# Where the rows of the normed activations begin in on-chip memory: 1088-byte rows against 1152-byte rows, all tiles behind them shifted

## The chip, the cores and the metric

The kernel runs on one core of a Trainium2 chip. The metric is the device time of one execution in microseconds (us). The kernel before was run three times: 1245.53, 1247.48 and 1249.95 us, median 1247.48 us. On-chip memory (SBUF) has 128 partitions; a tile occupies the same byte range in each of them, and this document is about where those ranges begin.

## The reference

The program computes four blocks in a row on an input of 256 tokens by 1024 channels, all in fp32. Cut to what matters here:

```
x = x + conformer_conv(rmsnorm(x))      # 1024 -> 2048, conv of width 31, 1024 -> 1024
x = x + swiglu(rmsnorm(x))              # 1024 -> 2 x 2816 -> 1024
x = x + dilated_attention(rmsnorm(x))
x = x + swiglu(rmsnorm(x))
cond = silu(c); mod = cond @ ada_w + ada_b        # shifts, scales, gates
x = x + g1 * (even_mixer(rmsnorm(x) * (1 + sc1) + sh1) @ w_out)
x = x + g2 * swiglu(rmsnorm(x) * (1 + sc2) + sh2)
x = x + g1' * (odd_mixer(rmsnorm(x) * (1 + sc1') + sh1') @ w_out')
x = x + g2' * swiglu(rmsnorm(x) * (1 + sc2') + sh2')
```

with `swiglu(h, wg, wu, wd) = (silu(h @ wg) * (h @ wu)) @ wd`. Nearly all arithmetic is in sixteen matrix products of activations with weights.

## The kernel before

**Layout of the data.** Activations lie transposed: channels on the 128 partitions, tokens along the row. A tensor of 1024 channels is 8 rows (`kt` = 0 to 7) of 256 tokens. Every fp32 operand of a big product is split into a high and a low part in the matrix unit's fp32r format: `HH` and `HL` for normed activations (two sets each, `[128, 8, TW]`), `GH` and `GL` for the gated activations of the feed-forward (`[128, 22, 256]`), `whi` and `wlo` for weights (six buffers each, one unit of eight 128x128 blocks per buffer). For a block of weights and a row of activations the TensorE queue runs three matmuls (line 528): weights high with activations high, weights high with activations low, weights low with activations high. The names in the profile put the activation first: `ps<-HH,whi`, `ps<-HL,whi`, `ps<-HH,wlo`, then the next block. I call these three a triple; the weights are the stationary operand and the row of activations the moving one.

**Products.** In order: pw1 (16 output tiles), pw2 (8), gu0 (44), dn0 (8), mixd (18), outd (8), gu1 (44), dn1 (8), mixe (23), oute (8), gu2 (44), dn2 (8), mixo (12), outo (8), gu3 (44), dn3 (8). The `gu` products are the gate and up projections, the `dn` products are the down projections and read `GH`/`GL` in 22 triples per output tile; all the others read `HH`/`HL` in 8 triples per tile (6 for outd). In mixe, gu2, mixo and gu3 the moving row has 258 columns instead of 256, since two columns behind the tokens carry the shift of the modulation (hence rows that are wider than 256). In six of mixd's tiles the roles are swapped (weights moving, activations stationary). The first two to four output tiles of a product ("lead") are interleaved: for each `kt` all lead tiles use the same row, so that 6 to 12 matmuls in a row read it; from then on tile follows tile, and each row is used for three matmuls. Orders differ in two products: outd goes through its rows as 0, 2, 4, 1, 3, 5 and oute as 0, 1, 4, 5, 2, 6, 3, 7.

**The other engines.** SyncE's queue streams the weights (`raw`, five buffers of 512 KB); ScalarE rounds each unit to `whi` (line 865), VectorE subtracts to `wlo` (line 1274), one unit after the other, five units ahead of TensorE. Between these, ScalarE and VectorE take the results out of PSUM, compute norms, gates and attention, and VectorE accumulates the modulation's sums (`aacc`). Each `whi` waits until TensorE has finished with the buffer.

**Placement.** Tiles are placed one behind the other in the order in which they are declared (`sb(...)`, lines 390 to 468), each rounded up to a multiple of 32 bytes; a group in a `with ExitStack() as st:` gives its place back at the end of the block, so that the next group begins where it began. The first buffer, `raw0`, begins at byte 16512, 128 beyond a multiple of 512, and so, because they are all multiples of 512 bytes long, does every `raw`, `whi`, `wlo` buffer, `X`, and `HH`, `HL`. With `TW` = 272 the rows of `HH` and `HL` are 1088 bytes apart. Beyond a multiple of 256 the rows then begin as follows (the pattern repeats after four):

```
row kt             0    1    2    3    4    5    6    7
HH, HL before    128  192    0   64  128  192    0   64   (bytes beyond a multiple of 256)
GH, GL before     64 for every row (base 181824, rows of 1024 bytes)
```

The ones among the small tiles that the change touches: `epsb`, `epse` and eight `bcol` tiles of one column each, 32 bytes apiece. VectorE writes a `bcol` from PSUM (lines 1499, 1618) and ScalarE or VectorE add it as a bias.

Of the kernel before, what the change touches and what calls it, by code (L numbers as in the profile page):

```python
# [7 lines left out]
F32 = mybir.dt.float32  # L8
# [5 lines left out]
P = 128  # L14
T = 256
# [2 lines left out]
KF = 22  # L18
EPS = 1e-6
UW = T + 28  # L20
TW = T + 16
NB = P + T
NR = 24
NEG = -1e30
# [360 lines left out]
def program(nc, wall, ada, x_in, vec_in, wq_in, row_in, rel_in, k128, kdist, koh, kmask, kbias, scratch, uscr, out):  # L385
    with ExitStack() as ctx:
        S = Signals(lambda name: ctx.enter_context(nc.semaphore("s_" + name)))

        def sb(name, shape, dt=F32, stack=ctx):
            return stack.enter_context(nc.sbuf_tensor(name, shape, dt))  # L390
# [3 lines left out]
        whi = [sb(f"whi{i}", [P, BLK * P], F32R) for i in range(RING)]  # L394
        wlo = [sb(f"wlo{i}", [P, BLK * P], F32R) for i in range(RING)]
        X = sb("X", [P, KD, T])
        HH = [sb(f"HH{i}", [P, KD, TW], F32R) for i in range(2)]
        HL = [sb(f"HL{i}", [P, KD, TW], F32R) for i in range(2)]
        RST = [sb(f"RST{i}", [P, T]) for i in range(2)]
# [2 lines left out]
        dist = sb("dist", [P, 384])  # L402
        vec, row = sb("vec", [P, NVEC]), sb("row", [P, NROW])
        MOD, GM, FG, cond = sb("MOD", [P, 96]), sb("GM", [P, 4, 8]), sb("FG", [P, 8]), sb("cond", [P, 8])
        epsb, epse = sb("epsb", [P, 1]), sb("epse", [P, 1])
        gqk, sc, rcol, lamt = sb("gqk", [P, 3]), sb("sc", [P, 8]), sb("rcol", [P, 2]), sb("lamt", [P, 2, 64])
        bcol = [sb(f"bcol{i}", [P, 1]) for i in range(8)]
        TMP = [sb(f"tmp{i}", [P, T]) for i in range(9)]
        TN = [sb(f"tn{i}", [P, T]) for i in range(2)]
        TS = [sb(f"ts{i}", [P, T]) for i in range(2)]  # L410
# [35 lines left out]
        SQC, SQD = sb("SQC", [P, T]), sb("SQD", [P, T])  # L446
        TS2 = [sb(f"tt{i}", [P, T]) for i in range(2)]
        with ExitStack() as st:
            GH, GL = sb("GH", [P, KF, T], F32R, st), sb("GL", [P, KF, T], F32R, st)
        with ExitStack() as st:  # L450
            oQ, oK, oV = sb("oQ", [P, 8, T], F32, st), sb("oK", [P, 4, T], F32, st), sb("oV", [P, 2, 256], F32, st)
# [7 lines left out]
        def V(name, i=0):  # L459
            c = VCOL[name] + i  # L460
            return vec[:, c:c + 1]

        def gain(i, nt):
            return (V("nm0", nt), V("nf0", nt), V("nm1", nt), V("nf1", nt), FG[:, nt:nt + 1], GM[:, 1, nt:nt + 1],
                    GM[:, 2, nt:nt + 1], GM[:, 3, nt:nt + 1])[i]
# [29 lines left out]
        def tensor_program():  # L495
# [41 lines left out]
            def total(i):  # L537

                pe.wait_ge(S.k128, 48)
                pe.wait_ge(S.sqa, 6 * (i + 1))  # L540
                pe.e.matmul(bank[7][:, 0:T], ones[:, :], SQA[:, :], start=True, stop=False)
                pe.wait_ge(S.sq, 8 * (i + 1))
                pe.then_inc(pe.e.matmul(bank[7][:, 0:T], ones[:, :], SQB[:, :], start=False, stop=True), S.tot)

            def norm_ready(i):
                def ready(kt):
                    pe.wait_ge(S.hl, 8 * i + kt + 1)
                    if i >= 4:
                        pe.wait_ge(S.sh, 2 * (i - 3))
                return ready  # L550
# [18 lines left out]
            def convolution():  # L569
# [17 lines left out]
                def after(nt):  # L587
# [8 lines left out]
                    if nt == 4:  # L596
# [4 lines left out]

                product("pw1", HH[NORM_SET[0]], HL[NORM_SET[0]], T, norm_ready(0), after,
                        lambda kt: total(0) if kt == KD - 1 else None)
# [17 lines left out]
                pe.then_inc(square, S.lnt)  # L621
                product("pw2", HH[LN_SET], HL[LN_SET], T, lambda kt: pe.wait_ge(S.lnl, kt + 1))

            def feed_forward(f):
# [6 lines left out]

                product(f"gu{f}", HH[NORM_SET[i]], HL[NORM_SET[i]], T + 2 if f >= 2 else T, norm_ready(i), after)
                product(f"dn{f}", GH, GL, T, lambda kt: pe.wait_ge(S.gl, KF * f + kt + 1),
# [15 lines left out]
            def dilated():  # L649
# [41 lines left out]
                def before(kt):  # L691
                    for w, hs in BEFORE_D.get(kt, ()):
                        step(w, hs)

                product("mixd", HH[NORM_SET[2]], HL[NORM_SET[2]], T, norm_ready(2), after)

                product("outd", HH[YD_SET], HL[YD_SET], T,
                        lambda kt: pe.wait_ge(S.dhl, 3 * (2 * (kt % 2) + 1) + kt // 2 + 1), None, before)
# [18 lines left out]
            def slotted(slot):  # L717

                def after(nt):
                    if nt == 1:  # L720
                        slot(2)
                    slot(2 * nt + 1)
                return dict(middle=lambda nt: slot(2 * nt), after=after)
# [7 lines left out]
            def even():  # L731
# [54 lines left out]
                def slot(s):  # L786
                    if s == 1:
                        total(4)
                        pe.wait_ge(S.sqa2, 6)
                        pe.wait_ge(S.amod, 3)  # L790
                        pe.e.matmul(bank[6][:, 0:T], ones[:, :], SQC[:, :], start=True, stop=False)
                        pe.wait_ge(S.sq2, 8)
                        pe.then_inc(pe.e.matmul(bank[6][:, 0:T], ones[:, :], SQD[:, :], start=False, stop=True), S.tot2)
                    project(TE, s)
                    if s == 16:
                        pe.wait_ge(S.twb, 1)
                        pe.wait_ge(S.sd, NORM_RST[4] + 2)
                    for w, k in AFTER_E.get(s, ()):
                        step(w, k)
# [6 lines left out]

                product("mixe", HH[NORM_SET[4]], HL[NORM_SET[4]], T + 2, norm_ready(4), **slotted(slot))
                product("oute", HH[YE_SET], HL[YE_SET], T, ready, None, lambda kt: slot(46 + PROD["oute"].order.index(kt)))
# [51 lines left out]
        def scalar_program():  # L860
# [3 lines left out]
            def act(o, i, func, sem, **kw):  # L864
                ac.then_inc(ac.e.activation(o, i, func, **kw), sem)  # L865
# [24 lines left out]
            def norm_high(i, nt):  # L890
# [3 lines left out]
                if i >= 4:  # L894
                    ac.wait_ge(S.gn, 3 if i < 6 else i - 2)
                act(HH[NORM_SET[i]][:, nt, 0:T], X[:, nt, :], ACT.Copy, S.hh, scale=gain(i, nt))

            def square(i, nt):
                streamed(i, nt)
                if nt in (0, KD - 1):  # L900
                    ac.wait_ge(S.tot, i)
                    act((SQB if nt else SQA)[:, :], X[:, nt, :], ACT.Square, S.sq)
                else:
                    m = 6 * i + nt - 1
                    ac.wait_ge(S.sqa, max(m - 1, 0))
                    act(TS[m % 2][:, :], X[:, nt, :], ACT.Square, S.sq)

            def square2(nt):
# [3 lines left out]
                else:  # L912
                    ac.wait_ge(S.sqa2, max(nt - 2, 0))
                    o = TS2[(nt - 1) % 2]
                act(o[:, :], X[:, nt, :], ACT.Square, S.sq2, scale=V("fin", nt))

# [352 lines left out]
        def vector_program():  # L1269
# [9 lines left out]
            def stt(o, a, s, b, op, op2, sem):  # L1279
                dv.then_inc(dv.e.scalar_tensor_tensor(out=o, in0=a, scalar=s, in1=b, op0=op, op1=op2), sem)  # L1280
# [34 lines left out]
            def norm_low(i, nt):  # L1315
                dv.wait_ge(S.hh, 8 * i + nt + 1)
                stt(HL[NORM_SET[i]][:, nt, 0:T], X[:, nt, :], gain(i, nt), HH[NORM_SET[i]][:, nt, 0:T].bitcast(F32),
                    ALU.mult, ALU.subtract, S.hl)
# [44 lines left out]
            def residual(name, i, scale, op, before=None):  # L1363
# [7 lines left out]
                for nt in range(p.tiles):  # L1371
# [12 lines left out]
                    else:  # L1384
                        dv.wait_ge(S.hl, 8 * j + nt + 1)
                    stt(X[:, nt, :], ps[:, 0:T], scale(nt), X[:, nt, :], op, ALU.add, S.ev)
                    if i is not None and nt == p.tiles - 1:
# [732 lines left out]
```

## Time and profile before

| | us |
|---|---|
| median of 3 runs (lowest to highest) | 1247.48 (1245.53 to 1249.95) |
| the profiled execution's own time | 1249.51 |
| its span, first to last instruction | 1248.2 |
| TensorE matmul busy / VectorE / ScalarE / GpSimd | 1186.6 / 926.3 / 657.7 / 80.1 |
| granted TensorE clock, mean share of full speed | 0.988 |

A busy matmul unit is not one at its peak: one matmul's record here lasts about 280 ns, but a new one starts every 113 to 120 ns, since they are pipelined. What counts is therefore the distance from one start to the next. It is read either from a timeline (starts to 10 ns) or from a view of one line's instructions over a stretch, which gives a count and the first and last start: the distance of the last from the first, divided by the count less one, is the time of one triple.

### The profile page before, as it was taken

The numbers are of one execution on the slowest core, as the hardware profiler recorded it, in microseconds if no ns is written. First come the engines' busy times: TensorE is split into PE (matmuls) and PEld (weight loads), VectorE is DVE, ScalarE is ACT, GpSimd is POOL, SyncE is SP. The second block draws the span as 40 slices with busy tenths as digits, with TensorE's granted clock in tenths as the row PEclk, the third lists the DMA queues.
The fourth block names the chain that finished last, engine by engine and source line by source line (L and its number), as shares of the span: only waits on it lengthen the run. The fifth ranks groups of instructions, "written<-read, shape, count | busy, mean of one in ns | idle before, by whom it ended". The sixth has DMA issues, their size and how long they took to land.

```text
span 1248.2 us, 24814 instructions
## 1 busy us (share of the span) xinstructions
PE 1186.6 (95%) x9914; PEld 1130.0 (91%) x9914; DVE 926.3 (74%) x1761; ACT 657.7 (53%) x1143; POOL 80.1 (6%) x91
## 2 busy tenths in 40 slices
PE   7898999999998999999997889999999899999999
PEld 7777999999987999999986779999998778999999
DVE  6646798878777888788788768888885565766653
ACT  6336654445445644446455776544445776544441
POOL 2010000001000100002100011000000222000000
PEclk9999999999999999999999999999999999999999
DMA  7862697878753588778744335887776432666561
GB/s 269 239 178 70 229 311 257 265 264 289 262 190 118 179 268 252 251 239 287 261 135 125 111 113 196 276 255 249 254 289 210 140 111 85 218 182 182 181 201 68
DMA packets 81270, 257.78 MB, mean 207 GB/s; under 512 B 9016, under 2 KB 22020, under 8 KB 81156
## 3 DMA queue, kind: packets, MB, share of 16 engines
q1 hardware_dynamic: 75396, 250.36, 60.9%
q10 hardware_dynamic: 5760, 5.83, 1.9%
q8 instruction: 79, 1.29, 0.4%
q14 instruction: 35, 0.29, 0.1%
HBM read 253.49 MB, written 2.67 MB: 205 GB/s over the span
## 4 chain that ended last, share of the span: by engine, by line
PE 79%; DVE 8%; ACT 4%; issue 3%; DMA 1%; POOL 1%; ACTq 0%; DVEq 0%; POOLq 0%
PE ps L528 71%; PE ps L579 2%; DVE wlo L1274 2%; PE ps L638 1%; PE ps L646 1%; PE ps L637 1%; PE ps L642 1%; DMA UR<-uscr 1%; DVE X L1280 1%; ACT whi L865 1%; DVE aacc L1280 1%; ACT oS L865 1%; ACT HH L865 1%; DVE HL L1280 1%; PE ps L560 1%
## 5 line engine op out<-in xcount | busy, mean ns | idle before, releaser
L528 PE MATMUL ps<-HH,whi 128*128 128x256 f32 (+1 forms) x2152 | 619.7, 288 | 17.8 <-DVE wlo L1274 8.2
L528 PE MATMUL ps<-HL,whi 128*128 128x256 f32 (+1 forms) x2152 | 611.4, 284 | 0.0
L528 PE MATMUL ps<-HH,wlo 128*128 128x256 f32 (+1 forms) x2152 | 610.7, 284 | 0.0
L865 ACT ACTIVATE whi<-raw 128x1024 fp32r<-128x1024 f32 (+1 forms) x364 | 382.3, 1054 | 340.5 <-PE ps L528 325.7
L1274 DVE TENSOR_TENSOR wlo<-raw,whi 128x1024 fp32r<-128x1024 f32 (+1 forms) x364 | 441.8, 1221 | 45.7 <-ACT whi L865 45.3
L528 PEld LDWEIGHTS ps<-HH,whi 128*128 128x128 f32 x2152 | 411.8, 191 | 34.9 <-issue 24.7
L528 PEld LDWEIGHTS ps<-HH,wlo 128*128 128x128 f32 x2152 | 412.6, 192 | 0.0
L528 PEld LDWEIGHTS ps<-HL,whi 128*128 128x128 f32 x2152 | 411.4, 191 | 0.4
L528 PE MATMUL ps<-GH,whi 128*128 128x256 f32 x704 | 195.6, 278 | 0.6 <-DVE bcol L1499 0.5
L528 PE MATMUL ps<-GL,whi 128*128 128x256 f32 x704 | 195.0, 277 | 0.0
L528 PE MATMUL ps<-GH,wlo 128*128 128x256 f32 x704 | 195.0, 277 | 0.0
L1280 DVE SCALAR_TENSOR_TENSOR aacc<-araw,cond,aacc 128x512 f32<-128x512 f32 x168 | 132.1, 786 | 3.4
L528 PEld LDWEIGHTS ps<-GH,whi 128*128 128x128 f32 x704 | 132.7, 189 | 2.1 <-DVE bcol L1499 0.9
L528 PEld LDWEIGHTS ps<-GL,whi 128*128 128x128 f32 x704 | 132.2, 188 | 0.0
L528 PEld LDWEIGHTS ps<-GH,wlo 128*128 128x128 f32 x704 | 132.2, 188 | 0.0
L1805 POOL TENSOR_TENSOR SQA<-SQA,ts 128x256 f32<-128x256 f32 x48 | 41.0, 855 | 717.7 <-ACT ts L865 717.1
L1498 DVE TENSOR_TENSOR tmp<-ps,RST 128x256 f32<-128x256 f32 x88 | 37.1, 422 | 48.3 <-PE ps L528 47.5
L1274 DVE TENSOR_TENSOR tmp<-ps,RST 128x256 f32<-128x256 f32 x104 | 43.6, 420 | 36.3 <-PE ps L528 35.8
L865 ACT ACTIVATE tmp<-tmp,bcol 128x256 f32<-128x256 f32 x74 | 36.9, 500 | 32.3 <-DVE bcol L1618 30.6
L865 ACT ACTIVATE GH<-tmp 128x256 fp32r<-128x256 f32 x88 | 35.6, 404 | 23.2 <-DVE tmp L1274 18.1
L1274 DVE TENSOR_TENSOR GL<-tmp,GH 128x256 fp32r<-128x256 f32 x88 | 36.8, 418 | 1.9 <-ACT GH L865 1.9
L1280 DVE SCALAR_TENSOR_TENSOR X<-ps,MOD,X 128x256 f32<-128x256 f32 x32 | 15.2, 478 | 30.7 <-PE ps L528 30.7
(220 smaller groups left out, 937.9 us busy)
## 6 DMA issues: line engine op xcount, KB each, us to landing
raw<-wall SPq DMA_DIRECT2D x363, 512.0 KB, 4.3
araw<-ada SPq DMA_DIRECT2D x96, 512.0 KB, 4.7
UR<-uscr ACTq DMA_DIRECT2D x32, 142.0 KB, 3.8
oBB<-kbias SPq DMA_DIRECT2D x16, 192.0 KB, 2.5
aTB<-scratch SPq DMA_DIRECT2D x12, 128.0 KB
uscr<-U ACTq DMA_DIRECT2D x8, 143.5 KB, 4.9
out<-X SPq DMA_DIRECT2D x8, 128.0 KB, 2.9
aTB<-scratch SPq DMA_DIRECT2D x12, 64.0 KB
```

What stands on the lines that cost most here:

```text
L528: ins = pe.e.matmul(o, l, r, start=(kt == p.order[0] and i == 0), stop=(kt == p.order[-1] and i == 2))
L560: ins = pe.e.matmul(bank[6][32 * i:32 * i + 32, :], ones[:, 0:32], aacc[(4 * b + i) % AACC][:, :], start=True, stop=True)
L579: ins = pe.e.matmul(bk[32 * r:32 * r + 32, 0:T], DG[j % 3][:, 8 * r + m, :], UR[j % 3][:, r, 4 * m:4 * m + T], start=(m == 0), stop=(m == 7))
L637: pe.e.matmul(bk[:, 0:128], q[:, 0:128], k[:, 0:128], start=True, stop=True)
L638: return pe.e.matmul(bk[:, 128:384], q[:, 128:256], k[:, 0:256], start=True, stop=True)
L642: ins = pe.e.transpose(bk[:, i * P:(i + 1) * P], s[:, i * P:(i + 1) * P], ident[:, :])
L646: pe.e.matmul(o, v(0), pt[:, 0:256], start=True, stop=False)
L865: ac.then_inc(ac.e.activation(o, i, func, **kw), sem)
L1274: dv.then_inc(dv.e.tensor_tensor(o, a, b, op), sem)
L1280: dv.then_inc(dv.e.scalar_tensor_tensor(out=o, in0=a, scalar=s, in1=b, op0=op, op1=op2), sem)
L1498: dv.e.tensor_tensor(t[:, :], ps[:, 0:T], rooted(name)[:, :], ALU.mult)
L1805: po.then_inc(po.e.tensor_tensor(o, a, b, op), sem)
```

## The change

The rows of `HH` and `HL` become 64 bytes longer: `TW` goes from 272 to 288 elements, 1152 bytes. A tile `half` of 64 bytes, which nothing reads or writes, is declared ahead of `HH`; another, `halfg`, ahead of `GH` and `GL`, in their own group. The ten one-column tiles are merged into two, `eps2` and `bcols`, and used by the same names through slices. No instruction is added, removed or moved on any engine, and no wait or semaphore changes.

```diff
-TW = T + 16
+TW = T + 32
...
         X = sb("X", [P, KD, T])
+        sb("half", [P, 16])
         HH = [sb(f"HH{i}", [P, KD, TW], F32R) for i in range(2)]
         HL = [sb(f"HL{i}", [P, KD, TW], F32R) for i in range(2)]
...
-        epsb, epse = sb("epsb", [P, 1]), sb("epse", [P, 1])
+        eps2, bcols = sb("eps2", [P, 2]), sb("bcols", [P, 8])
+        epsb, epse = eps2[:, 0:1], eps2[:, 1:2]
+        bcol = [bcols[:, i:i + 1] for i in range(8)]
         gqk, sc, rcol, lamt = sb("gqk", [P, 3]), sb("sc", [P, 8]), sb("rcol", [P, 2]), sb("lamt", [P, 2, 64])
-        bcol = [sb(f"bcol{i}", [P, 1]) for i in range(8)]
...
         with ExitStack() as st:
+            sb("halfg", [P, 16], F32, st)
             GH, GL = sb("GH", [P, KF, T], F32R, st), sb("GL", [P, KF, T], F32R, st)
```

## Rows read from the trace of the kernel before

**Rows 1.** The page: busy time by engine, and shares of the chain by line

```profile
PE 1186.6 (95%) x9914; PEld 1130.0 (91%) x9914; DVE 926.3 (74%) x1761; ACT 657.7 (53%) x1143; POOL 80.1 (6%) x91
...
PE ps L528 71%; PE ps L579 2%; DVE wlo L1274 2%; PE ps L638 1%; PE ps L646 1%; PE ps L637 1%; PE ps L642 1%; DMA UR<-uscr 1%; DVE X L1280 1%; ACT whi L865 1%; DVE aacc L1280 1%; ACT oS L865 1%; ACT HH L865 1%; DVE HL L1280 1%; PE ps L560 1%
```

**Rows 2.** Waits, whole run: engine, line, releaser: total us, times, longest

```profile
ACT whi L865 <- PE ps L528: 325.7, 222, 10.0
```

**Rows 3.** Groups by line and shape: count | busy us, mean ns | idle before

```profile
L528 PE MATMUL ps<-HH,whi 128*128 128x256 f32 x1168 | 333.6, 286 | 14.8 <-DVE wlo L1274 8.2 <-DVE HL L1274 5.2 <-DVE X L1280 1.2
...
L528 PE MATMUL ps<-HH,whi 128*128 128x258 f32 x984 | 286.2, 291 | 3.0 <-DVE bcol L1618 2.0 <-DVE X L1280 1.0
...
L528 PE MATMUL ps<-GH,whi 128*128 128x256 f32 x704 | 195.6, 278 | 0.6 <-DVE bcol L1499 0.5 <-DVE tmp L1274 0.2
```

**Rows 4.** Line 528 in gu0, 142 to 249 us: count, ns min/median/max, first to last start

```profile
L528 PE MATMUL ps<-HL,whi x303: 279/282/283, 141.7 to 248.9; 128*128 128x256 f32 x152
```

**Rows 5.** The same in gu3, 1078 to 1178 us

```profile
L528 PE MATMUL ps<-HH,whi x280: 280/282/285, 1077.8 to 1178.0; 128*128 128x258 f32 x140
```

**Rows 6.** The same in dn1, 551.5 to 609 us

```profile
L528 PE MATMUL ps<-GH,whi x170: 276/276/276, 551.3 to 608.7; 128*128 128x256 f32 x170
```

**Rows 7.** The same in dn2's first six tiles, 894.3 to 940.5 us

```profile
L528 PE MATMUL ps<-GL,whi x131: 281/281/281, 894.1 to 940.0; 128*128 128x256 f32 x131
```

**Rows 8.** The same in dn2's last two tiles, 942 to 956 us

```profile
L528 PE MATMUL ps<-GH,wlo x40: 276/276/283, 942.0 to 955.7; 128*128 128x256 f32 x40
```

**Rows 9.** Timeline of TensorE in pw1's lead: start us, duration us, instruction

```profile
15.40 0.28 PE L528 MATMUL ps<-HH,whi 128*128 128x256 f32 x1
...
16.08 0.28 PE L528 MATMUL ps<-HH,whi 128*128 128x256 f32 x1
...
17.50 0.28 PE L528 MATMUL ps<-HH,whi 128*128 128x256 f32 x1
...
18.92 0.28 PE L528 MATMUL ps<-HH,whi 128*128 128x256 f32 x1
```

**Rows 10.** The same in outd's lead, rows 1, 3, 5 in turn

```profile
404.61 0.28 PE L528 MATMUL ps<-HH,whi 128*128 128x256 f32 x1
...
405.32 0.28 PE L528 MATMUL ps<-HH,whi 128*128 128x256 f32 x1
...
406.02 0.28 PE L528 MATMUL ps<-HH,whi 128*128 128x256 f32 x1
...
406.73 0.29 PE L528 MATMUL ps<-HH,whi 128*128 128x256 f32 x1
```

**Rows 11.** The same in outo's lead, row 5 behind a wait

```profile
1035.48 0.28 PE L528 MATMUL ps<-HL,whi 128*128 128x256 f32 x1
...
1036.30 0.28 PE L528 MATMUL ps<-HH,wlo 128*128 128x256 f32 x1
```

**Rows 12.** The same in gu3's lead (258 columns), rows 1 and 3

```profile
1058.91 0.28 PE L528 MATMUL ps<-HH,whi 128*128 128x258 f32 x1
...
1059.98 0.28 PE L528 MATMUL ps<-HH,whi 128*128 128x258 f32 x1
...
1061.07 0.28 PE L528 MATMUL ps<-HH,whi 128*128 128x258 f32 x1
...
1062.15 0.28 PE L528 MATMUL ps<-HH,whi 128*128 128x258 f32 x1
```

**Rows 13.** The same in one later tile of gu3

```profile
1073.45 0.28 PE L528 MATMUL ps<-HH,whi 128*128 128x258 f32 x1
...
1074.17 0.28 PE L528 MATMUL ps<-HH,whi 128*128 128x258 f32 x1
...
1074.55 0.28 PE L528 MATMUL ps<-HH,whi 128*128 128x258 f32 x1
...
1075.97 0.28 PE L528 MATMUL ps<-HH,whi 128*128 128x258 f32 x1
```

**Rows 14.** Instructions that write or read HH, bcol, and line 579

```profile
L865 ACT ACTIVATE HH<-X,vec x32: 490/509/513, 4.4 to 422.6; 128x256 fp32r<-128x256 f32 x32
...
L1499 DVE COPY bcol<-ps x88: 141/148/151, 773.5 to 1185.7; 128x1 f32<-128x1 f32 x88
...
L579 PE MATMUL ps<-UR,DG x512: 376/379/472, 36.6 to 98.1; 128*32 128x256 f32 x171
```

## The prediction

> **What bounds the kernel now.** First the page: TensorE is busy 95% of the span, and 71% of the chain that ended last is line 528, the matmuls of the big products [rows 1]. ScalarE waits 325.7 us in all for TensorE to free a weight buffer, and hardly for anything else in that line [rows 2], so the weight stream runs ahead, and a faster or slower matmul goes straight into the time. The reader is to see that no other engine needs to be looked at for a change that moves no instruction.
>
> Then the groups by shape. A matmul on HH has a mean of 286 ns at 256 columns and 291 at 258, one on GH 278 [rows 3], though HH and GH matmuls at 256 columns do the same work. The means are of pipelined records, so I read distances between starts. In gu0 302 triples take 107.2 us, 355.0 ns each: 118.3 ns a matmul [rows 4]. In dn1 169 triples take 57.4 us, 339.6 ns each: 113.3 a matmul [rows 6]; dn0 and dn3 show the same. In gu3 279 triples take 100.2 us: 119.7 a matmul [rows 5]. So HH matmuls are 4 to 5 ns slower than GH ones, and there are many of them: 3 x 1168 at 256 columns and 3 x 984 at 258 [rows 3].
>
> **What the placement has to do with it.** GH is not fast everywhere. In dn2's first six tiles, same tiles, same places, 130 triples take 45.9 us, 117.7 ns a matmul, every record 281 ns [rows 7]; behind the wait that follows them the records are 276 ns again [rows 8]. A stream over equally placed rows thus has a fast rate (113.3) and a slow one (117.7), and keeps the one it falls into. Next, which placements know the fast rate. In a product's lead several matmuls in a row read one row of HH. In pw1's lead the last six on row 3 (64 bytes beyond a multiple of 256) take 0.68 us, the first two starts shown, 113.3 each [rows 9]; the twelve on row 4 (128 beyond) take 1.42 us, 118.3 each, and the twelve on row 5 (192 beyond) again 1.42 us, and these never come down [rows 9]. Behind a wait, where the stream starts afresh, row 5 in outo runs 7 matmuls in 0.82 us, 117.1 [rows 11], also slow. I find thirteen such runs of six or more on rows that lie 192 beyond, from pw1's to outo's (the two shown), and none reaches 113.3; on rows 64 beyond, and on GH and GL, which also lie 64 beyond, both rates occur. So what counts here is the place within 256 bytes, not within 128: 64 can be fast, 192 is slow.
>
> **The change part by part.** Nothing is added to any queue; everything is in the addresses.
>
> HH and HL move by 64 bytes and get rows of 1152 bytes: 128 + 64 = 192, and 1152 is 4 x 256 + 128, so the rows lie 192, 64, 192, 64, ... beyond a multiple of 256. All are 64 beyond a multiple of 128, as announced.
>
> GH and GL: HH and HL add 4 x 8 x 64 = 2048 bytes, `half` 64, the merged columns give back 7 x 32 + 32 = 256, `halfg` adds 64: 1920 bytes in all. 181824 + 1920 = 183744, which is 192 beyond a multiple of 256. They too stay 64 beyond a multiple of 128, but leave the place where the fast rate was seen. The weights stay where they are.
>
> *Term 1, the gated products.* Fast today are dn0, dn1, dn3 (8 x 22 x 3 = 528 matmuls each) and dn2's last two tiles (132): 1716. If rows 192 beyond have only the slow rate, each costs 117.7 - 113.3 = 4.4 ns more [rows 6, 7]: +7.6 us, all on the path. Bounds: if they keep the fast rate 0, and -1.7 if dn2's 396 slow ones become fast too. I take +7.6, by the thirteen runs.
>
> *Term 2, HH at 256 columns.* 3504 matmuls, at 118.3 today [rows 4]. outd's order happens to give exactly the new sequence: rows 1, 3, 5 lie 192, 64, 192 beyond. Its lead runs the 18 matmuls in 2.12 us, 117.8 each [rows 10]; the run on the row at 64 stays slow when it comes from a slow one. So -0.5 ns each: -1.8 us. Bounds: 113.3 for all, -17.5 us, and 118.3 again, 0.
>
> *Term 3, HH at 258 columns.* 2952 matmuls, at 119.7 today [rows 5]. Leads: row 1 (192) nine in 1.07 us, 118.9; row 3 (64) nine in 1.08, 120.0 [rows 12]. In a later tile, each row used three times: row 1 and the one behind it 120.0, row 3 126.7 (0.38 us for three), the twelve behind it 118.3 [rows 13]. Taking the odd rows at lead rates gives 119.4; with row 3 at 126.7 and the other three at 119 it gives 120.9. Neither has the new steps between rows, so I take the middle, about 120.1: +1.0 us. Bounds: 114.2 (113.3 x 258 / 256), -16.2 us, and 120.9, +3.5.
>
> *The rest.* The 144 matmuls of mixd with swapped roles read HH as weights, too few for a microsecond. ScalarE writes to HH took 490 to 513 ns over all eight rows [rows 14], so its rows' places show no cost there worth a bound over 32 x 0.02 = 0.7 us, and TensorE hides it. VectorE's copies to bcol took 141 to 151 ns at eight different places [rows 14]; packing them costs nothing visible, hidden as well except in the mixers. The taps' moving rows start at 16-byte steps and have a median of 379 with a minimum of 376 [rows 14]: moving them, and the attention's tiles, is worth at most 3 ns x 512 = 1.5 us either way; I take 0.
>
> *A rule against the rows.* The fast rate is 113.3 ns for 256 columns, the slow one 117.7, at unchanged shape and clock [rows 6, 7]. The Trainium skill (TensorE: Matmul & The Clock Gate, "Part 2: What happens when you issue a matmul") gives the gap between warm matmuls as columns / 2.4 GHz plus about 2.5 ns, 109.2 ns here, and says that loading the next weights takes nothing from the running matmul, since each has its own read port. By that no address matters and the change would do nothing; the two rates in this trace speak against it.
>
> *Sum.* 7.6 - 1.8 + 1.0 = +6.8 us. Against the profiled execution's 1249.5 that is 1256.3. The median of the runs is 2.0 lower, so I forecast **1254.3 us**.
>
> **Rivals.**
>
> *A, the forecast: 192 beyond is slow, the gated products lose the fast rate.* Own range: term 1 of 6.5 to 8, term 2 of -4 to 0, term 3 of -1.2 to +3.5, rest within 1.5: +1 to +12 at most, 1249 to 1259.5. Chance 0.53.
>
> *B, 128 is what counts.* Then the trouble of HH is only the step from a row at 0 to one at 64 beyond 128, and with equal rows all run like GH: -17.5 - 16.2 - 1.7 = -35 us, 1212. For it: GH's rows all equal, HH's not. Against it: the thirteen runs at 192, long enough to settle, that did not. Chance 0.17.
>
> *C, addresses hardly matter.* The two rates come from how the stream restarts after a wait, as in dn2 where the place did not change [rows 7, 8]. Then nothing moves but which stretch is slow: between -1.7 and, if one more dn turns slow, +2.3 us; 1247.5. Against: the ordered differences within one lead [rows 9]. Chance 0.17.
>
> *D, half a win.* Alternating rows fall into the fast rate on every second row: (113.3 + 117.7) / 2 = 115.5 at 256 columns, -2.8 x 3504 = -9.8 us, as much again in half at 258, -5, with the gated products' +7.6: -7, 1240. For: runs on row 3 come down within six matmuls [rows 9]. Against: outd [rows 10], and only three matmuls a row. Chance 0.13.
>
> **How the numbers follow.** A measurement of this kernel tells a change from none beyond about 0.3%, 3.7 us. Faster by more: B 0.17, D 0.10, together 0.27. Within: C 0.15, D 0.03, the low end of A 0.05: 0.23. Slower by more: A 0.48, C 0.02: 0.50. The range leaves out B: from D's 1240 less its spread to the top of A, 1236 to 1261.
>
> **What would show it.** In dn0, dn1, dn3 the records of line 528: 281 ns and triples of 353 ns if A or D is right, 276 and 340 if B or C. In gu0 and gu1 triples of 353 to 354 by A, 340 by B, 355 by C, about 346 by D. In gu3 about 360 by A. The prediction is wrong if GH at 192 beyond keeps 276 ns, or if the alternating rows of HH come below 350 ns a triple.

## The result and the profile after

| | before | after |
|---|---|---|
| median of the runs, us | 1247.56 (20 runs, 1238.97 to 1254.93) | 1252.22 (20 runs, 1246.47 to 1256.83) |
| profiled execution, us | 1249.51 | 1252.52 |
| its span, us | 1248.2 | 1251.2 |
| mean granted clock in it | 0.988 | 0.989 |

After over before is 1.0044, with a 95% interval of 1.0025 to 1.0062: 3.1 to 7.7 us slower. The forecast difference of +6.8 us lies inside; the middle, +5.5 us (0.44% of 1247.6), is 1.3 less.

The page of after first: busy time of each engine, and shares of the chain. TensorE grew by 2.3 us and still makes 71% of the chain with the line of the big products (531 now, 528 before) [rows 1].

```profile
PE 1188.9 (95%) x9914; PEld 1131.2 (90%) x9914; DVE 927.6 (74%) x1761; ACT 657.1 (53%) x1143; POOL 80.7 (6%) x91
...
PE ps L531 71%; DVE wlo L1277 2%; PE ps L582 1%; ACT whi L868 1%; PE ps L641 1%; PE ps L649 1%; PE ps L640 1%; DVE X L1283 1%; DMA uscr<-U 1%; PE ps L645 1%; DMA UR<-uscr 1%; DVE aacc L1283 1%; ACT oS L868 1%; ACT HH L868 1%; DVE HL L1283 1%
```

The waits of after (engine, line, releaser: total us, times, longest). ScalarE waits 5.4 us more for TensorE to free a weight buffer than in [rows 2], so the weight stream has as much slack as before, and slower matmuls are not hidden.

```profile
ACT whi L868 <- PE ps L531: 331.1, 223, 10.2
```

The groups of after by line and shape (busy us, mean ns of one, idle before). Against [rows 3], HH at 256 columns went from 286 to 285 ns, at 258 from 291 to 292, GH from 278 to 280: three small moves in two directions.

```profile
L531 PE MATMUL ps<-HH,whi 128*128 128x256 f32 x1168 | 332.3, 285 | 14.8 <-DVE wlo L1277 8.0 <-DVE HL L1277 5.2 <-DVE X L1283 1.3
L531 PE MATMUL ps<-HH,whi 128*128 128x258 f32 x984 | 287.1, 292 | 3.1 <-DVE bcols L1621 2.0 <-DVE X L1283 1.1
...
L531 PE MATMUL ps<-GH,whi 128*128 128x256 f32 x704 | 197.4, 280 | 0.6 <-DVE bcols L1502 0.5 <-DVE tmp L1277 0.2
```

The means mix stretches, so again line 531 by stretch, one of its three matmuls each (count, ns min/median/max, first to last start): gu0, dn1, dn2's first six tiles, gu3.

```profile
L531 PE MATMUL ps<-HH,wlo x307: 277/277/279, 141.7 to 248.8; 128*128 128x256 f32 x154
...
L531 PE MATMUL ps<-GH,whi x164: 279/279/279, 551.3 to 608.9; 128*128 128x256 f32 x164
...
L531 PE MATMUL ps<-GL,whi x129: 278/279/279, 896.6 to 941.8; 128*128 128x256 f32 x129
...
L531 PE MATMUL ps<-HH,wlo x278: 278/282/289, 1077.8 to 1177.8; 128*128 128x258 f32 x139
```

gu0: 306 triples in 107.1 us, 350.0 ns each, where [rows 4] had 355.0. dn1: 163 triples in 57.6 us, 353.4, where [rows 6] had 339.6. dn2: 128 triples in 45.2 us, 353.1, as in [rows 7]. gu3: 277 triples in 100.0 us, 361.0, where [rows 5] had 359.1.

The granted clock does not explain the two rates: in before it was full (1.00, the number behind the count in brackets) in dn2's slow stretch and in the fast one behind it, and so it was in after's gu0 and dn1.

```profile
894.30:940.00 45.70, 45.70 (x390) 1.00 0.76 266
941.30:956.00 14.70, 14.70 (x133) 1.00 0.62 201
```

The same read for every product, as the mean distance between starts of neighbouring matmuls, gives what I call the account below. Only distances under 140 ns are taken, so stalls are left out, and the difference of the means is multiplied by the number of these distances (2097 for the 2112 gated matmuls, some 3380 for the 3504):

| term | predicted | ns a matmul, before to after | us |
|---|---|---|---|
| 1, gated products, 2112 matmuls | +7.6 | 114.2 to 117.8 | +7.5 |
| 2, HH at 256 columns, 3504 | -1.8 | 118.2 to 116.9 | -4.5 |
| 3, HH at 258 columns, 2952 | +1.0 | 119.9 to 120.3 | +1.3 |
| sum | +6.8 | | +4.3 |

The spans differ by 3.0 us, so -1.3 us are left. Some -0.5 of them is mixd's 144 matmuls with swapped roles, which the prediction had put at nothing: they went from 118.0 to 113.7 ns each. The other -0.8 lies in stalls and small products, and no row names a cause for it.

### The profile page after: what moved, and what is told of

The parts are those of the page before. It is cut to its first block, busy times and chain, and to the rows that moved or that the text cites. A ratio compares the mean times of both kernels' runs of the same rounds, so it can differ in the third digit from the quotient of the medians.

```text
span 1251.2 us, 24814 instructions
## 1 busy us (share of the span) xinstructions
PE 1188.9 (95%) x9914; PEld 1131.2 (90%) x9914; DVE 927.6 (74%) x1761; ACT 657.1 (53%) x1143; POOL 80.7 (6%) x91
## 4 chain that ended last, share of the span: by engine, by line
PE 78%; DVE 9%; ACT 5%; issue 3%; DMA 2%; POOL 1%; ACTq 0%; DVEq 0%; POOLq 0%
PE ps L531 71%; DVE wlo L1277 2%; PE ps L582 1%; ACT whi L868 1%; PE ps L641 1%; PE ps L649 1%; PE ps L640 1%; DVE X L1283 1%; DMA uscr<-U 1%; PE ps L645 1%; DMA UR<-uscr 1%; DVE aacc L1283 1%; ACT oS L868 1%; ACT HH L868 1%; DVE HL L1283 1%
## 5 line engine op out<-in xcount | busy, mean ns | idle before, releaser
L868 ACT ACTIVATE whi<-raw 128x1024 fp32r<-128x1024 f32 (+1 forms) x364 | 382.3, 1054 | 345.2 <-PE ps L531 331.1
L868 ACT ACTIVATE tmp<-tmp,bcols 128x256 f32<-128x256 f32 x74 | 36.9, 500 | 32.3 <-DVE bcols L1621 30.7
```

## Experiments

The theory, in the form that the experiments led to: what decides is the distance, modulo 256 bytes, between a row that TensorE reads and the weights, which lie 128 beyond a multiple of 256. The prediction had spoken of the row's place alone, and the expectations call the common part "theory 1". A place allows certain rates, and at a restart, behind a wait, a stream falls into one of them. Rival one: only the restart decides, and all four gated products turned slow by accident. Rival two: the row's own place counts, whatever the weights'. Places are given as bytes beyond a multiple of 256.

### The gated rows alone, taken back and added

e1_gated_back is after with GH and GL returned to 64.

```diff
-            sb("halfg", [P, 16], F32, st)
+            sb("halfg", [P, 48], F32, st)
```

> The changed kernel with 128 bytes more ahead of GH and GL, so that they lie 64 beyond a multiple of 256 again; HH and HL as in the change (192, 64, 192, 64, ...). Theory 1 (the place within 256 bytes sets the rate): records of the dn products back at 276 ns, triples of 340 ns, at least in dn0, dn1, dn3; gu0 and gu1 stay at about 350 ns a triple as in the changed kernel. The time is 7.7 us under the changed kernel's: 1244.5, some 3 us under the kernel before. Theory 2 (the slow rate is an accident of how a stream restarts): no connection with the 128 bytes, dn stays at 353 ns a triple, 1252. Rival 3 (it is the place within 128 bytes, or the change's other tiles): the same as theory 2, 1252.

e2_gated_alone is before with GH and GL moved to 192 and nothing else.

```diff
+            sb("halfg", [P, 32], F32, st)
             GH, GL = sb("GH", [P, KF, T], F32R, st), sb("GL", [P, KF, T], F32R, st)
```

> The kernel before with 128 bytes ahead of GH and GL and nothing else: they lie 192 beyond a multiple of 256. Theory 1: dn0 to dn3 at 353 ns a triple throughout, all other products unchanged (355 in gu0, 359 in gu3), time +7.6 us: 1255. Theory 2: no change, 1247.5.

Measured: e1 1247.61 us, ratio to before 1.0008 [0.9983, 1.0034]; e2 1255.82 us, ratio 1.0072 [1.0047, 1.0097]. Line 531 of e1 in dn0, then line 529 of e2 in gu0 and in dn1 (columns as above):

```profile
L531 PE MATMUL ps<-GH,whi x148: 275/276/277, 259.8 to 309.7; 128*128 128x256 f32 x148
```

```profile
L529 PE MATMUL ps<-HH,wlo x302: 279/282/283, 141.8 to 248.7; 128*128 128x256 f32 x151
...
L529 PE MATMUL ps<-GL,whi x114: 278/279/280, 559.8 to 599.7; 128*128 128x256 f32 x114
```

e1: 147 triples in 49.9 us, 339.5: the fast rate came back with the place, in all four gated products. e2: HH untouched (301 triples in 106.9 us, 355.1), dn1 at 113 triples in 39.9 us, 353.1, and all four gated products at 117.8 ns. By the account, e2 has +7.5 in term 1 and 0.1 or less elsewhere; e1 has -3.8 in term 2, -1.7 in term 1 (dn2 was fast throughout) and +0.9 in term 3. Term 1 is thus shown both ways. e2's median agrees with the expected 1255. e1's is 3 us above the expected 1244.5: its account of -4.6 us against before is there in its profiled execution (1243.95 us at a granted clock of 0.989, 5.6 less than before's), and not in its median; the last section comes back to that.

### What the distance is measured from

e3_all_128 moves everything from the raw weights on by 128 bytes, the weights included; e4_weights_128 moves the weights whi and wlo alone (a second shift restores the rest modulo 256).

```diff
 e3, ahead of raw:      + sb("shift", [P, 32])
 e4, ahead of whi:      + sb("shift", [P, 32])
 e4, ahead of X:        + sb("shift2", [P, 32])
```

> The kernel before with 128 bytes ahead of the first buffer, so that every tile lies 128 further, the weights too (0 beyond a multiple of 256 instead of 128, GH 192 instead of 64). Theory 1a (the distance between the row and the block of weights counts, within 256 bytes): every product as before, dn 340 ns a triple, 1247. Theory 1b (the row's own place counts): dn at 353 ns, 1255.

> The kernel before with 128 bytes ahead of the weights' split buffers and 128 behind them: only whi and wlo move within 256 bytes (0 beyond instead of 128), every row of activations stays. Theory 1a (distance to the weights): dn slow, 353 ns a triple, 1255. Theory 1b (the row's own place): dn 340 ns, 1247.

Measured, one execution each: e3 1244.33 us, e4 1257.97. Line 529 of e3 in dn1, then line 530 of e4 in dn0 and in dn1:

```profile
L529 PE MATMUL ps<-GH,wlo x119: 275/276/277, 559.8 to 599.9; 128*128 128x256 f32 x119
```

```profile
L530 PE MATMUL ps<-GH,whi x143: 279/279/279, 259.7 to 309.9; 128*128 128x256 f32 x143
...
L530 PE MATMUL ps<-GL,whi x148: 276/276/276, 559.7 to 609.7; 128*128 128x256 f32 x148
```

In e3 GH lies at 192, as in after, and is fast (118 triples in 40.1 us, 339.8), as in the other three gated products (dn2's last tile excepted, 117.8 ns a matmul). In e4 GH lies at 64, as in before, and dn0 is slow (142 triples in 50.2 us, 353.5), as are dn2 and dn3. With before and after, that makes all four combinations of two places of the row and two of the weights, and the rate goes with the distance between them: rival two falls. The last line belongs to neither side: e4's dn1 took the fast rate (147 triples in 50.0 us, 340.1) at the slow distance.

### Every row of the 256-column products at 64

e5_rows_1024 is before, with the 256-column products going through views with rows of 1024 bytes at 64 in the same buffers.

```diff
+        HN, LN = ([b[:, 48:48 + KD * T].rearrange("p (k t) -> p k t", t=T) for b in B] for B in (HHB, HLB))
...
-                product("pw1", HH[NORM_SET[0]], HL[NORM_SET[0]], T, norm_ready(0), after,
+                product("pw1", NH[0], NL[0], T, norm_ready(0), after,
```

(HHB and HLB are the buffers of HH and HL without rows; NH and NL are these views for products 0 to 3 and the old rows for the wider ones. The lines that write HH and HL use the same views.)

> The kernel before, where the products with 256 columns (pw1, pw2, gu0, mixd, outd, gu1, oute, outo) address HH and HL with rows of 1024 bytes that all begin 64 beyond a multiple of 256, in the same memory; the products with 258 columns keep rows of 1088 bytes, and no tile moves. Theory 1 (the distance of the row from the block of weights, within 256 bytes, sets which rates there are, and 64 knows the fast one): 340 ns a triple wherever the fast rate is caught, so up to 4.9 ns x 3504 matmuls = 17 us less: 1230 to 1236; if a stream is caught in the slow rate, 353 there, and the gain of that product is 0.5 ns a matmul. Rival (HH is slower than GH for another reason, such as its writers or its being renewed during the product): 353 to 355, 1246.

> The kernel with 1024-byte rows at 64 once more, for the rates of its streams in a second profiled execution. The two later kernels with the same rows had gu0 at 117.5 ns a matmul and gu1 at 113.4, so the fast rate is caught by chance: each of gu0, gu1, pw2 and outd at 113.4 or 117.7, not all of them fast as the first time; time between 1233 (all fast) and 1243.

Measured: e5 1240.75 us, ratio 0.9948 [0.9924, 0.9971], faster than both kernels, but 5 us above the expected 1230 to 1236; e12, the same kernel again, one execution, 1238.2. The page and the waits of e5, line 532 of e5 in gu0, then that of e12 in gu0 and in dn2:

```profile
PE 1170.0 (95%) x9914; PEld 1112.8 (90%) x9914; DVE 925.7 (75%) x1761; ACT 657.6 (53%) x1143; POOL 80.8 (7%) x91
```

```profile
ACT whi L869 <- PE ps L532: 306.6, 214, 10.2
```

```profile
L532 PE MATMUL ps<-HH,wlo x289: 276/276/276, 141.8 to 239.7; 128*128 128x256 f32 x145
```

```profile
L532 PE MATMUL ps<-HH,wlo x289: 276/276/276, 141.8 to 239.8; 128*128 128x256 f32 x145
...
L532 PE MATMUL ps<-GL,whi x126: 281/281/281, 885.8 to 930.0; 128*128 128x256 f32 x126
```

288 triples in 97.9 us: 339.9 in gu0, the rate that only the gated products had before. Not every product got it: pw1 had 115.6 ns a matmul, oute 117.1 and outo 116.9, which is why term 2 falls short of the 17 us that were possible. TensorE's busy time falls by 16.6 us against [rows 1] and ScalarE's wait by 19.1 against [rows 2]; the account gives -14.0 us in term 2 and -1.7 in term 1, and the two spans differ by 15.2 (1248.2 to 1233.0). The medians differ by only 4.3 (1245.06 to 1240.75) and the ratio says 6.5: the profiled execution, 1234.31 us, lies near the lowest of the 12 runs, 1233.21. e12 keeps gu0 fast but has dn2 slow at 125 triples in 44.2 us, 353.6, and outd at 117.6.

### A map of places

e6_gated_map gives GH and GL another place in each gated product (0, 32, 96, 128); e7_all_64 puts all rows at 64, with rows of 1280 bytes for 258 columns; e8_places_258 is e7 with the 258-column products at 128, 192, 32, 0 and the gated ones at 160, 224, 64, 192; e11_192_for_258 is e7 with the 258-column rows at 192. To make room, e7, e8 and e11 also merge the one-column tiles and place some scratch tiles over others, and e8 has two load buffers for the modulation instead of three; their times are therefore less clean than their rates.

```diff
 e6: +            GHV, GLV = ([b[:, o:o + KF * T].rearrange("p (k t) -> p k t", t=T) for o in (48, 56, 8, 16)] for b in (GHB, GLB))
 e7: +TW = T + 64
 e8: +        AT = {4: 0, 5: 16, 6: 40, 7: 32}
 e11: -        sb("half", [P, 48])
 e11: +        sb("half", [P, 16])
 e11: -        HN, LN = ([b[:, 0:0 + KD * T]...
 e11: +        HN, LN = ([b[:, 32:32 + KD * T]...
```

> The kernel before with GH and GL read and written at another place in each feed-forward: dn0 at 0, dn1 at 32, dn2 at 96, dn3 at 128 bytes beyond a multiple of 256 (the weights lie 128 beyond). Theory 1: each place has rates of its own; by the lead's runs of HH rows 0 gives about 356 ns a triple, 128 about 358 to 360; 32 and 96 were never seen, between 340 and 360. Rival (only the step between rows matters, not the constant place): all four at 340.

> All moving rows 64 beyond a multiple of 256: the products with 258 columns get rows of 1280 bytes, those with 256 columns rows of 1024 bytes, GH and GL as before. The room for it comes from merging the one-column tiles and from placing four scratch rows of the sums and one of the dilated attention's buffers over scratch that is free at that time. Theory 1: the products with 256 columns as in the run with 1024-byte rows, 340 to 353 ns a triple. For 258 columns it does not say which rate a constant row gives: between 342.5 (340 x 258 / 256) and the lead rows' 357 to 360; so 1213 to 1236. Rival: nothing gained, 1246.

> Rows of 258 columns with a constant place, 1280 bytes apart: mixe at 128, gu2 at 192, mixo at 32, gu3 at 0 beyond a multiple of 256 (the run with all at 64 had 120.8 ns a matmul in gu2 and gu3). GH and GL in dn0 at 160, dn1 at 224, dn2 at 64, dn3 at 192. One of the modulation's three load buffers is left out to make room, which may cost VectorE waits but not TensorE's rate. Theory 1: with 258 columns each matmul leaves the next one two columns further off, so that no place keeps a fast rate: 118.5 to 121 everywhere. Rival: some place knows 114.2. For the dn products: dn3 353 ns a triple, dn2 340 or 353, the other two between 350 and 360.

> The two best places together: 256-column rows 1024 bytes apart at 64 beyond a multiple of 256, GH and GL at 64, and 258-column rows 1280 bytes apart at 192, where gu2 took 118.8 ns a matmul against 119.8 in the kernel before. Theory 1: gu2 and gu3 118.8, mixe and mixo 119 to 120, the others 113.3 where the fast rate is caught and 117.7 where not; 3 us less than the run with 1024-byte rows, 1238. Rival (the 118.8 was one more accident of a restart): gu2 or gu3 above 119.5, 1241 or more.

Measured: e6 1255.06 us and e8 1251.5, one execution each; e7 1243.25, ratio 0.9979 [0.9952, 1.0005], so not clear of before and above the expected 1213 to 1236; e11 1239.35, ratio 0.9951 [0.993, 0.9973]. The line of the products in each: e6 in dn0 and dn3; e7 in gu0, gu1 and gu3; e8 in gu2 and gu3; e11 in gu0 and gu3.

```profile
L529 PE MATMUL ps<-GL,whi x142: 279/281/285, 259.7 to 309.9; 128*128 128x256 f32 x142
...
L529 PE MATMUL ps<-GL,whi x148: 280/283/287, 1191.8 to 1244.7; 128*128 128x256 f32 x148
```

```profile
L535 PE MATMUL ps<-HL,whi x270: 281/281/281, 149.8 to 244.8; 128*128 128x256 f32 x135
...
L535 PE MATMUL ps<-HH,wlo x230: 276/276/276, 441.8 to 519.6; 128*128 128x256 f32 x115
...
L535 PE MATMUL ps<-HH,wlo x222: 280/283/289, 1089.8 to 1169.9; 128*128 128x258 f32 x111
```

```profile
L535 PE MATMUL ps<-HH,whi x170: 277/282/283, 779.8 to 840.0; 128*128 128x258 f32 x170
...
L535 PE MATMUL ps<-HH,wlo x219: 282/283/283, 1079.8 to 1159.7; 128*128 128x258 f32 x110
```

```profile
L535 PE MATMUL ps<-HH,wlo x270: 280/281/282, 149.7 to 244.8; 128*128 128x256 f32 x135
...
L535 PE MATMUL ps<-HH,whi x225: 277/283/286, 1079.8 to 1159.8; 128*128 128x258 f32 x113
```

As triples: e6 356.0 at 0 and 359.9 at 128; e7 353.2 in gu0, 339.7 in gu1, both at 64, and 362.4 in gu3; e8 356.2 at 192 and 366.5 at 0; e11 353.5 in gu0 and 357.1 in gu3. Mean distances, ns a matmul, with all rows of a product at one place and the weights at 128:

| place | 256 columns | 258 columns |
|---|---|---|
| 0 | 118.7 | 122.2 |
| 32 | 117.3 | 120.2 |
| 64 | 113.3 or 117.7 | 120.8 |
| 96 | 118.4 | |
| 128 | 120.0 | 120.5 |
| 160 | 116.7 | |
| 192 | 117.8, seldom 113.4 | 118.8 to 119.3 |
| 224 | 120.0 | |

Most places rest on one product in one run, and the product changes with the place, so steps under 1 ns in this table aren't settled. Seen at 256 columns is the rate of 113.3 at 64, and seldom at 192. That the other six places don't know it isn't shown: each had one gated product in one profile, and 192 shows it in 2 of 17. 258 columns found no such rate at the five places tried. By the account e7 wins 9.4 us in term 2 and gives 2.6 back in term 3; e11, with term 3 at -2.0, has 8.4 in term 2, since gu0, pw2 and outd fell into the slow rate.

### Both kernels again, unchanged

> The kernel before once more, for the rate of each product in a second profiled execution. If the rate a stream falls into at places that know both is an accident of its restart, dn0 to dn3 are each 340 or 353 ns a triple, not in the same pattern as in the first profile (340, 340, mostly 353, 340); the HH products stay within 0.3 ns a matmul.

> The changed kernel once more. By theory 1 all of dn0 to dn3 at 353 ns a triple again; if 192 beyond knows the fast rate as well, as one product of the run with the weights moved showed, one or more of the four may come at 340. gu0 and gu1 between 340 and 354.

Measured, one execution each: e9 1239.82 us, e10 1250.69. Line 528 of e9 in dn2's first tiles, then line 531 of e10 in gu0 and dn1:

```profile
L528 PE MATMUL ps<-GH,whi x107: 276/276/276, 893.8 to 929.8; 128*128 128x256 f32 x107
```

```profile
L531 PE MATMUL ps<-HH,whi x302: 278/280/283, 141.8 to 248.2; 128*128 128x256 f32 x151
...
L531 PE MATMUL ps<-GH,whi x154: 275/276/277, 552.7 to 604.8; 128*128 128x256 f32 x154
```

The same code at the same addresses doesn't always take the same rate: dn2 of before, 353 in [rows 7], is 339.6 in e9 (106 triples in 36.0 us), and after has dn1 fast (340.5) and gu0 at 353.5 instead of 350.0 in e10. By the account e10 stands against before at +5.2 us in term 1, -2.6 in term 2 and +0.9 in term 3: +3.5 in all.

## Why the prediction was right, and where it was not

**What bounds the kernel** held: matmuls that cost more or less went into the time, and ScalarE's wait followed them in both directions (325.7, 331.1, 306.6 us).

**The layout arithmetic** held: after has HH at 94400 and GH at 183744 bytes, both 192 beyond a multiple of 256.

**Term 1** was right in size, +7.5 for +7.6 us, and is the cause of the loss: e2 has it alone and is 0.47 to 0.97% slower, e1 takes it back and has no loss left. Its reason was too strict. "64 can be fast, 192 is slow" should read: over all the profiles, products of GH at before's distance from the weights ran fast in most of their tiles in 30 of 33 cases (the other three were dn2, in before, e7 and e12), at after's distance in 2 of 17 (both dn1). Thirteen slow leads made a good forecast and not a law. The place was also the wrong word, as e3 and e4 show: the distance to the weights counts.

**Term 2** was mis-sized: -1.8 predicted, -4.5 measured, past the -4 that A's own range allowed; e10 has -2.6. The term took outd's lead, where six matmuls in a row read one row, for a stream in which the row changes after every three. In after's gu0 the three distances on a row at 192 come to 354 ns together and those on a row at 64 to 346. In e10 gu0 is at 117.7, the rate that the prediction had read in outd [rows 10]. So the lead named one of two rates of this sequence. Why alternating rows have a rate of 350 ns a triple too is open; e8's dn0, with all rows at 160, has it as well (116.7 a matmul). The prediction had named triples below 350 at the alternating rows as a sign of being wrong: gu0 stands just on that mark, and oute, with a mean of 116.4 ns a matmul or 349.2 a triple, just below it. The prediction's rule that a row at 64 stays slow when it comes from a slow one did not hold in after's gu0 (346 ns against 354).

**Term 3** was right within its uncertainty: +1.3 for +1.0, and +0.9 in e10. Its working was loose, so part of this is luck: 120.1 against 119.7 gives +1.2, not +1.0, and the case with 126.7 counts the row at 64 once in four rows, where after the change every second row lies there. Counted so it would be 122.9 and +9.3 us, which did not come.

**The rest at nothing** held, but for the -0.5 us of mixd's swapped tiles, by the rows of after, which answer to [rows 14]: ScalarE's writes to HH, VectorE's copies into bcols, and the taps.

```profile
L868 ACT ACTIVATE HH<-X,vec x32: 491/510/512, 4.2 to 423.6; 128x256 fp32r<-128x256 f32 x32
...
L1502 DVE COPY bcols<-ps x88: 145/148/151, 775.2 to 1186.4; 128x1 f32<-128x1 f32 x88
...
L582 PE MATMUL ps<-UR,DG x512: 376/379/634, 37.0 to 97.1; 128*32 128x256 f32 x171
```

**The rivals.** B (only 128 counts) is out: all rows lie 64 beyond a multiple of 128, gu0 takes 350 and not 340, and GH at 192 lost its rate. C (addresses hardly matter) named a real mechanism, the draw at a restart, but not its odds: e2 moves two buffers and changes nothing but the four gated products. D (half a win) had the sign of term 2 right and its size at twice what came: alternating rows gave 350.0 or 353.5 a triple and not 346. Its -5 us at 258 columns did not come (+1.3). A's own terms add up to between -0.2 and +13 us, a little wider than the +1 to +12 that it states; what was measured lies inside both. The signs that were named came as A has them in dn (353 ns a triple), above A's 360 by 1 in gu3, and between A and D in gu0.

The Trainium skill (TensorE: Matmul & The Clock Gate, "Part 2: What happens when you issue a matmul") gives the gap of warm matmuls as columns / 2.4 GHz plus about 2.5 ns, from which I estimate 109.2 ns at 256 columns, and names no effect of addresses; it adds that the formula has no budget for the weight loads. The fastest rate in any run here is 113.3 ns, and e5's 0.5% was won by addresses alone; the measurement decides.

## What to carry to other kernels

When a kernel is bound by matmuls that each load new weights, read the distance between starts, not the mean duration, and compare streams of one shape: if they differ by some 4%, as 117.7 and 113.3 do here, look at the distance between the moving rows and the weights modulo 256 bytes. Here rows that all lie 64 bytes before the weights' place were the best (e5, 0.5% off the whole kernel); being equal modulo 128 wasn't enough, since after's 256-column products on HH got only 350 to 353.5 ns a triple from it and the gated ones lost. A placement shifts the odds of a rate and doesn't fix it, so a gain of this kind needs several runs, or several profiles, before it is believed.

## What was not expected of the hardware

- One stream of matmuls of 256 columns has several steady rates. At constant rows the profiles have 340, 350, 352, 353.3, 355, 356 and 360 ns a triple, by the table of places. No common step shows in them, and the mechanism stays open.
- The distance matters with the roles swapped as well. In mixd's swapped tiles the weights are the moving operand and a row of HH the stationary one. They took 118.0 ns a matmul in before, 117.8 in e5, e7 and e8 (rows at 64), and 113.7 and 113.6 in after and e10 (rows at 192 and 64 in turn). In e5 the moving operand lies 64 bytes beyond the stationary one, as in after's gated products, and is slow as they are. In after it lies 64 short of it and 64 beyond it in turn, and why that is fast throughout no run here shows.
- The time follows the granted clock even within runs of one kernel on one core: it lay between 0.980 and 0.993 in the profiled executions. A line through all runs gives 8.7 us more (standard error 0.6) for each 0.01 less of it. At equal clock that line puts after at +4.8 us, e1 at -1.6, e2 at +7.1, e5 at -10.4, e7 at -5.7 and e11 at -8.1 against before, each with a standard error of 0.9 or less. Over their runs e1, e5 and e7 had 0.9855 to 0.9864 where before had 0.9891, which accounts for some 2 to 3 us by which their medians fall short of the account; why they got the lower clock, no run here shows. A higher rate of matmuls can't be all of it, since e2, slower than before, had 0.9864 as well. What the line leaves of the account (e5 -10.4 for -15.7, e1 -1.6 for -4.6) stays open; other runs having drawn slower rates than the profiled one is a guess.
- Two columns more take away more than their own time: 258 columns ran at 118.8 ns at best, 5.5 more than the 113.3 of 256, where two columns at that rate would be 0.9.
